# Half tiles filled with zeros at the hybrid mixers' branch projections, and a new order of emptying and outputs at the ends of the hybrid and neighbourhood attentions

## The chip, the cores and the metric

One core of one Trainium2 chip runs the whole program. The time is device microseconds of one execution, median of three: 2294.79 us (2292.48 to 2295.53).

## The reference

One sequence of 256 tokens with 1024 features goes through four transformer layers in fp32. First part: two layers, each a mixer, a cross attention to a memory of 256 tokens and a feed-forward network with a three-tap convolution. The first layer's mixer is the even one (grouped attention and mLSTM), the second layer's the odd one (neighbourhood attention and differential attention). Second part: two layers, each a half-step feed-forward network, a hybrid mixer, a cross attention and another feed-forward network. The change touches the odd mixer and both hybrid mixers:

```python
def odd_mixer(h, w_in, ...):
    qc, kc, vc, qd, kd, vd = split_cols(h @ w_in, OD_SIZES)
    yc = neighbourhood_attention(qc, kc, vc, na_rpb)         # 8 heads of 64
    yd = differential_attention(q12[0], q12[1], k12[0], k12[1], vd, lam, t5_table)
    return concatenate([merge(yc), merge(yd)]) @ w_out

def hybrid_mixer(h, positions, w_in, ...):
    o_fox = fox_attention(fq, fk, fv, log_f)                 # 6 heads of 64: 384 rows
    o_dsa = dsa_sparse_attention(dq, dk, dv, q_idx, k_idx, w_idx, topk)  # 5 heads: 320 rows
    o_sb = stick_breaking_attention(sq, sk, sv)              # 5 heads: 320 rows
    g = sigmoid(gates)
    merged = g[0] * (o_fox @ w_fox_out) + g[1] * (o_dsa @ w_dsa_out) + g[2] * (o_sb @ w_sb_out)
    return merged @ w_out
```

## The kernel before

Activations lie feature by token: a tile is 128 features by 256 tokens. Every matrix product in fp32 is made of three matmuls of parts: the weight is split in a rounded part `whi` and a remainder `wlo`, the activation in `x_hi` and `x_lo`, and the products lo x hi, hi x lo and hi x hi are summed (`product`, L882, L883, L885; in `as_it_comes`, which takes the input tile by tile as it becomes ready, L923, L924, L927). An output tile with eight input tiles is 24 matmuls of 256 columns, one with three input tiles is 9.

Weights come in chunks of up to 2048 columns. SP loads a chunk into one of three `raw` slots (L760) as soon as the slot's former chunk is split; ACT makes `whi` (L1398); `wlo` is a subtraction on DVE (L1843) or, for chunks used inside the attention stages, on POOL (L850, four pieces of 512 columns). A memory chunk is no weight: it replaces the activations `x_hi`, `x_lo` by the normalised memory (ACT L1391, DVE L1839), which must wait until the last unit that reads the old activations is done.

A *unit* is one output of two tiles in one of two PSUM banks, used in turn; unit u may start when unit u-2 has been emptied (`bank_free`). DVE empties gates and queries (L1870), residuals (L1874), tokens (L1861) and the merging of branches (L1879, and the addition L1883 or L1886); ACT empties the memory's keys and values (L1416).

An attention stage is a loop over slots: in slot i PE makes the scores of head group i, then the units that `fill` lists for this slot, the values of group i-2 (L1185) and the transposes of group i-1 (L1171). ACT makes the exponentials of group i (L1641, or the logarithms for the stick-breaking groups), rounds the chunks that `fill` asks for, and copies the transposed probabilities of group i-1 (`back`, L1673). DVE makes maxima and normalisations of group i, then the subtractions and emptyings that `fill` asks for, and last `output(i-2)`: it rounds the attention's output into `x_hi` (L2215) and subtracts into `x_lo` (L2217). Each engine works strictly in this written order. `fill={slot: (end, emptied, ahead)}` means: PE emits units below `end`, the other engines empty units below `emptied`, and chunks are rounded and subtracted up to `ahead` beyond the last unit's (2 where nothing stands).

The hybrid attention has nine groups: 0 to 2 fox, 3 to 5 sparse (dsa), 6 to 8 stick-breaking (sb). Below, F0 to F3 are the units of the fox projection (slots 5 and 6), G9 to G11 the last gates (slots 7 and 8), M0 to M3 those of the dsa projection (slots 9 and 10), S0 to S3 those of the sb projection in the linear stage that follows (`feeds`), W0 to W3 those of `w_out`. dsa and sb have 320 input rows: two whole tiles and a half one of 64 rows. Both halves lie in tile 5 of the output activations, dsa's in rows 0 to 63, sb's in rows 64 to 127, and the matmuls of the half tile contract 64 rows. Each branch has four units of two tiles, so eight output tiles.

In the odd mixer, N0 to N5 are the last units of `od_w_in`, K0 to K3 the memory's keys and values, H0 to H3 the first half of `od_w_out`. K0 comes right after the neighbourhood attention, before a barrier of the stages.

## Time and profile before

| | us |
|---|---|
| median of three | 2294.79 |
| the profiled execution's own time | 2294.97 |
| its span | 2293.2 |
| PE busy | 2203.7 (96%) |
| PE weight load busy | 2112.2 (92%) |
| DVE busy | 1504.9 (66%) |
| ACT busy | 1108.0 (48%) |
| POOL busy | 355.9 (16%) |

The profile is one execution. Busy time is the time in which at least one instruction of an engine runs; the share is an average over stages with quite different limits. The granted clock is the share of TensorE's 2.4 GHz: 1.00 or 0.50 in a stretch. Times of rows are counted from the span's start. In this trace the neighbourhood attention ends at about 547 us, the first hybrid mixer's attention at about 1285 us and the second's at about 1992 us.

### The profile page before, as it was taken

Reading aid. Unit: us, or ns where it says so; the run is one execution under the profiler, and the core shown is the slowest. Engines: PE = TensorE matmul, PEld = TensorE weight load, DVE = VectorE, ACT = ScalarE, POOL = GpSimd, SP = SyncE. Lnnn points to the kernel's source line nnn. Section 1 sums busy time; section 2 is a strip of 40 time slices with the busy share of each in tenths; the row PEclk is TensorE's granted clock in tenths of the full one; section 3 lists DMA queues with packets and bytes.
Section 4 is the critical chain, followed back from the end, with each engine's and each line's share of the span. In section 5 each row is a group of like instructions: output and inputs, shape, how many; then the busy total and the mean of one; then the engine's idle time right before and its main releaser. Section 6 shows DMA issues by size and latency. Waiting matters only on the chain.

```text
span 2293.2 us, 40427 instructions
## 1 busy us (share of the span) xinstructions
PE 2203.7 (96%) x17458; PEld 2112.2 (92%) x17458; DVE 1504.9 (66%) x2210; ACT 1108.0 (48%) x1335; POOL 355.9 (16%) x300
## 2 busy tenths in 40 slices
PE   8988999998799999999999999999999999999998
PEld 7777899997689999999988799999999998799998
DVE  6656787843578787567766657657656566657655
ACT  5345654544465445335646455335334456455333
POOL 2760000055000000000645120000000015320000
PEclk9989999999999999999999999999999999999999
DMA  8653355543245555546643354555555653355552
GB/s 280 181 165 111 111 188 198 176 158 117 92 131 168 200 174 189 189 166 184 195 143 104 124 182 163 195 176 184 184 184 167 175 166 105 117 171 169 185 184 92
DMA packets 316964, 375.13 MB, mean 164 GB/s; under 512 B 27255, under 2 KB 283011, under 8 KB 315635
## 3 DMA queue, kind: packets, MB, share of 16 engines
q1 hardware_dynamic: 311635, 354.88, 47.4%
q0 software_dynamic: 3424, 11.50, 1.8%
q10 hardware_dynamic: 1728, 6.17, 0.7%
q8 instruction: 138, 2.26, 0.4%
q14 instruction: 39, 0.32, 0.0%
HBM read 363.34 MB, written 9.18 MB: 162 GB/s over the span
## 4 chain that ended last, share of the span: by engine, by line
PE 85%; DVE 7%; ACT 3%; issue 2%; DMA 1%; SPq 1%; DVEq 0%; POOL 0%; ACTq 0%
PE banks L882 24%; PE banks L885 23%; PE banks L883 23%; PE banks L923 3%; PE banks L924 3%; PE banks L927 3%; DVE wlo L1843 2%; PE banks L1147 1%; DMA raw<-in_ev_w_in 1%; PE banks L1185 1%; ACT whi L1398 1%; PE banks L1171 1%; PE banks L1045 1%; SPq L760 1%; PE banks L892 0%
## 5 line engine op out<-in xcount | busy, mean ns | idle before, releaser
L882 PE MATMUL banks<-x_hi,wlo 128*128 128x256 f32 (+1 forms) x4344 | 1101.5, 286 | 18.2 <-DVE gt L1879 6.9
L883 PE MATMUL banks<-x_lo,whi 128*128 128x256 f32 (+1 forms) x4344 | 1092.3, 284 | 0.0
L1398 ACT ACTIVATE whi<-raw 128x2048 fp32r<-128x2048 f32 (+3 forms) x340 | 637.7, 1879 | 601.1 <-PE banks L885 551.8
L882 PEld LDWEIGHTS banks<-x_hi,wlo 128*128 128x128 f32 (+1 forms) x4344 | 838.4, 193 | 37.0 <-issue 19.8
L883 PEld LDWEIGHTS banks<-x_lo,whi 128*128 128x128 f32 (+1 forms) x4344 | 839.0, 193 | 0.0
L1843 DVE TENSOR_TENSOR wlo<-raw,whi 128x2048 fp32r<-128x2048 f32 (+4 forms) x290 | 652.3, 2260 | 120.6 <-ACT whi L1398 120.3
L885 PE MATMUL banks<-x_hi,whi 128*128 128x256 f32 x4344 | 687.9, 284 | 0.0
L885 PEld LDWEIGHTS banks<-x_hi,whi 128*128 128x128 f32 x4344 | 595.8, 193 | 3.2
L850 POOL TENSOR_TENSOR wlo<-raw,whi 128x512 fp32r<-128x512 f32 x192 | 251.7, 1347 | 1121.4 <-ACT whi L1398 1121.4
L923 PE MATMUL banks<-x_hi,wlo 128*128 128x256 f32 (+1 forms) x624 | 170.5, 305 | 13.9 <-DVE gt L1879 5.0
L924 PE MATMUL banks<-x_lo,whi 128*128 128x256 f32 (+1 forms) x624 | 163.9, 295 | 0.0
L923 PEld LDWEIGHTS banks<-x_hi,wlo 128*128 128x128 f32 (+1 forms) x624 | 127.6, 204 | 20.8 <-issue 6.1
L2409 DVE TENSOR_TENSOR wk<-banks,norm_scale 128x512 f32<-128x512 f32 x132 | 90.9, 689 | 74.2 <-PE banks L885 69.6
L924 PEld LDWEIGHTS banks<-x_lo,whi 128*128 128x128 f32 (+1 forms) x624 | 127.7, 205 | 0.4
L805 POOL TENSOR_SCALAR gt<-gt,cols 128x256 f32<-128x256 f32 x32 | 42.6, 1343 | 544.8 <-DVE gt L1921 544.8
L2448 DVE CAST x_hi<-wk 128x512 fp32r<-128x512 f32 x66 | 28.2, 427 | 131.6 <-PE banks L885 130.6
L2427 DVE SCALAR_TENSOR_TENSOR wk<-wk,cols 128x255 f32<-128x255 f32 x176 | 73.4, 480 | 39.4 <-ACT wk L1763 38.7
L882 PE MATMUL banks<-whi,x_lo 128*128 128x256 f32 (+3 forms) x400 | 96.7, 282 | 0.0
L883 PE MATMUL banks<-wlo,x_hi 128*128 128x256 f32 (+3 forms) x400 | 95.3, 279 | 0.0
L927 PE MATMUL banks<-x_hi,whi 128*128 128x256 f32 (+1 forms) x632 | 92.9, 285 | 0.0
L1763 ACT ACTIVATE wk<-wk,cols 128x256 f32<-128x256 f32 x88 | 45.7, 590 | 92.0 <-DVE wk L2409 92.0
L1447 ACT ACTIVATE x_hi<-xT,con,cols 128x256 fp32r<-128x256 f32 x112 | 60.9, 590 | 59.7 <-DVE xT L1874 49.8
...
## 6 DMA issues: line engine op xcount, KB each, us to landing
...
```

What stands on the lines that cost most here:

```text
L850: m = eng.tensor_tensor(wlo[s][:, at:at + PIECE], full[:, at:at + PIECE], whi[s][:, at:at + PIECE].bitcast(F32), ALU.subtract)
L882: eng.matmul(out, a[1], b[0], start=first and i == 0, stop=False, skip_group_check=True)
L883: eng.matmul(out, a[0], b[1], start=False, stop=False, skip_group_check=True)
L885: m = eng.matmul(out, a[0], b[0], start=False, stop=last and i == len(operands) - 1, skip_group_check=True)
L923: eng.matmul(bank[:, o], a[1], b[0], start=i == 0 and k0 + k == 0, stop=False, skip_group_check=True)
L924: eng.matmul(bank[:, o], a[0], b[1], start=False, stop=False, skip_group_check=True)
L927: m = eng.matmul(bank[:, o], a[0], b[0], start=False, stop=k == n - 1, skip_group_check=True)
L1398: eng.activation(whi[s % SETS][:, 0:ch["n"]], raw[i % SLOTS][:, 0:ch["n"]], ACT.Copy).then_inc(S["weights_hi"], 1)
L1447: eng.activation(X[nm["buf"]][0][:, k, :], xT[:, k, :], ACT.Identity, scale=cols[:, nm["gain"] + k:nm["gain"] + k + 1], bias=C("zero")).th ...
L1843: eng.tensor_tensor(wlo[s][:, 0:n], full[:, 0:n], whi[s][:, 0:n].bitcast(F32), ALU.subtract).then_inc(S["weights_split"], 1)
L2409: return eng.tensor_tensor(wk[:, half, :].rearrange("p (n c) -> p n c", c=SEQ), bank[:, :].rearrange("p (n c) -> p n c", c=SEQ), norms, AL ...
L2427: m = eng.scalar_tensor_tensor(out=o, in0=wk[:, half, i * SEQ:(i + 1) * SEQ][:, src], scalar=cols[:, w:w + 1], in1=o, op0=ALU.mult, op1=AL ...
```

## The change

Three things are changed. One: in a branch projection with a half tile, the other 64 rows of that weight tile are loaded with zeros (a new input of 64 x 512 zeros, one more DMA per chunk), and the matmuls contract all 128 rows. The dsa units then read rows 64 to 127 of tile 5 too, so they wait for group 6's output (`dsa = n_of["att"] + 7`).

Two: in the hybrid attention DVE empties all units of a slot but the last right after its subtractions and the top-k rounds, ahead of `output(i-2)`; in the last slot `output` comes ahead of the subtractions. In the stage that follows ACT rounds the chunk for W1 ahead of parts 2 and 3, and DVE makes parts 2 to 7 of the merged activations together after S3.

Three: in the neighbourhood attention `output(i-2)` comes ahead of the slot's `fill`, unit N5 moves from slot 2 to slot 3, K0's weights are loaded and rounded ahead of the memory chunk, and in slot 4 ACT copies the transposed probabilities ahead of rounding.

```diff
@@ row_chunk @@
                     pieces.append((v[p0:p0 + r, at, :], w[r0:r0 + r, col:col + n]))
-                    own.append((at, p0, p0 + r))
+                    if r < P:
+                        pieces.append((v[HD - p0:P - p0, at, :], io["zeros"][:, 0:n]))
+                    own.append((at, 0, P))
@@ memory_units @@
-        def memory_units(layer, buf, last_unit):
+        def memory_units(layer, buf, last_unit, keys_first=False):
+            wkv, done = io["ca_w_kv"][layer], COLS if keys_first else 0
+            units = features(wkv, buf, 0, done, 0, "plain")
             c = mem_chunk(layer, buf, last_unit)
-            wkv = io["ca_w_kv"][layer]
-            us = enroll(features(wkv, buf, 0, 512, 0, "plain")) + enroll(values(wkv, buf, 512, 512, 0, "plain"))
+            units += features(wkv, buf, done, 512 - done, done // P, "plain")
+            us = enroll(units) + enroll(values(wkv, buf, 512, 512, 0, "plain"))
@@ odd_mixer, neighbourhood attention @@
-                      fill={0: (N[4], N[3]), 1: (N[5], N[4]), 2: (N[5] + 1, N[5]), 3: (N[5] + 1, N[5] + 1)})
-            K = memory_units(1, b, N[5])
+                      fill={0: (N[4], N[3]), 1: (N[5], N[4]), 2: (N[5], N[5]), 3: (N[5] + 1, N[5], 2), 4: (N[5] + 1, N[5] + 1, 3)})
+            K = memory_units(1, b, N[5], keys_first=True)
             H = enroll(residual_half(wo, o, 0))
-            stages[-1]["fill"][4] = (N[5] + 1, N[5] + 1, 3)
@@ hybrid_mixer @@
-            fox, dsa = n_of["att"] + 3, n_of["att"] + 6
+            fox, dsa = n_of["att"] + 3, n_of["att"] + 7
@@ ACT, linear @@
+                    if feeds is not None and i == 1:
+                        split_upto(two_on(units[2]["chunk"]))
                     if feeds is not None:
                         parts_hi(feeds, 2 * i, 2 * i + 2)
@@ ACT, in_units @@
+                    back_first = st.get("outputs_first") and i == len(units)
+                    if back_first:
+                        back(i - 1)
                     fill(st, i)
-                    if 0 <= i - 1 < len(units):
+                    if 0 <= i - 1 < len(units) and not back_first:
                         back(i - 1)
@@ DVE, linear @@
-                    if feeds is not None and i:
-                        parts_lo(feeds, 2 * i - 2, 2 * i)
+                    if feeds is not None and i in (1, 3):
+                        parts_lo(feeds, i - 1, i + 1)
...
-                    parts_lo(feeds, 6, 8)
+                    parts_lo(feeds, 4, 8)
@@ DVE, in_units @@
+                    outputs_first = st.get("outputs_first") or i > len(units)
+                    if outputs_first and i >= 2:
+                        output(i - 2)
                     fill(st, i)
...
+                    if top and i in st["fill"]:
+                        evac_upto(st["fill"][i][0] - 1)
-                    if i >= 2:
+                    if i >= 2 and not outputs_first:
                         output(i - 2)
```

DVE around G11, M0 and M1 in the second hybrid mixer (the first reads the same), from `output(6)` of 64 rows to M3's merging, before:

```order
L2215 CAST x_hi<-banks 64x256 [waits att_o]
L2217 TENSOR_TENSOR x_lo<-banks,x_hi 64x256 [waits dve_step]
L1870 SCALAR_TENSOR_TENSOR gt<-banks,norm_scale 128x512 [waits mem_stored,lin_ready] x2
L1843 TENSOR_TENSOR wlo<-raw,whi 128x1536 [waits weights_hi]
L2215 CAST x_hi<-banks 128x256 [waits att_o]
L2217 TENSOR_TENSOR x_lo<-banks,x_hi 128x256 [waits dve_step]
L1879 SCALAR_TENSOR_TENSOR gt<-gt,banks 128x512 [waits gated,lin_ready]
L1883 TENSOR_TENSOR gt<-gt 128x512 [waits lin_free]
L1879 SCALAR_TENSOR_TENSOR gt<-gt,banks 128x512 [waits gated,lin_ready,dve_step]
```

And after (the changed kernel's lines 1851, 1878, 1887, 1891, 2223, 2225 are 1843, 1870, 1879, 1883, 2215, 2217 of before):

```order
L1878 SCALAR_TENSOR_TENSOR gt<-banks,norm_scale 128x512 [waits mem_stored,lin_ready]
L2223 CAST x_hi<-banks 64x256 [waits att_o]
L2225 TENSOR_TENSOR x_lo<-banks,x_hi 64x256 [waits dve_step]
L1878 SCALAR_TENSOR_TENSOR gt<-banks,norm_scale 128x512 [waits mem_stored,lin_ready]
L1851 TENSOR_TENSOR wlo<-raw,whi 128x1536 [waits weights_hi]
L1887 SCALAR_TENSOR_TENSOR gt<-gt,banks 128x512 [waits gated,lin_ready]
L1891 TENSOR_TENSOR gt<-gt 128x512 [waits lin_free]
L2223 CAST x_hi<-banks 128x256 [waits att_o,dve_step]
L2225 TENSOR_TENSOR x_lo<-banks,x_hi 128x256 [waits dve_step]
L1887 SCALAR_TENSOR_TENSOR gt<-gt,banks 128x512 [waits gated,lin_ready]
```

G10 is now emptied ahead of `output(6)`, and M0 ahead of `output(7)`.

DVE from the last `output` of the attention to W1's chunk, before (L2012 makes the lo parts of the merged activations):

```order
L1843 TENSOR_TENSOR wlo<-raw,whi 128x1536 [waits weights_hi,dve_step]
L2215 CAST x_hi<-banks 128x256 [waits att_o]
L2217 TENSOR_TENSOR x_lo<-banks,x_hi 128x256 [waits dve_step]
L1843 TENSOR_TENSOR wlo<-raw,whi 128x2048 [waits weights_hi]
```

And after:

```order
L2223 CAST x_hi<-banks 128x256 [waits att_o,dve_step]
L2225 TENSOR_TENSOR x_lo<-banks,x_hi 128x256 [waits dve_step]
L1851 TENSOR_TENSOR wlo<-raw,whi 128x1536 [waits weights_hi]
L1851 TENSOR_TENSOR wlo<-raw,whi 128x2048 [waits weights_hi]
```

`output(8)` passes the subtraction of S2's chunk.

ACT in the neighbourhood attention, from the exponentials of group 1 to the barrier, before (L1641 the exponentials, L1673 `back`, L1391 the memory, L1398 weights):

```order
L1673 ACTIVATE wk<-banks 128x1024 [waits att_pt]
L1641 ACTIVATE wk,stat<-wk,stat 128x256 [waits att_pt,att_max]
L1641 ACTIVATE wk,stat<-wk,stat 128x256 x3
L1673 ACTIVATE wk<-banks 128x1024 [waits att_o,att_pt]
L1641 ACTIVATE wk,stat<-wk,stat 128x256 [waits att_pt,att_max]
L1641 ACTIVATE wk,stat<-wk,stat 128x256 x3
L1673 ACTIVATE wk<-banks 128x1024 [waits att_o,att_pt]
L1391 ACTIVATE x_hi<-raw 128x2048 [waits lin_ready,weights_loaded1]
L1398 ACTIVATE whi<-raw 128x2048 [waits lin_ready,weights_loaded2]
L1398 ACTIVATE whi<-raw 128x2048 [waits lin_ready,weights_loaded0]
L1673 ACTIVATE wk<-banks 128x1024 [waits att_o,att_pt]
```

And after (lines 1646, 1678, 1394, 1401 are 1641, 1673, 1391, 1398 of before):

```order
L1401 ACTIVATE whi<-raw 128x2048 [waits lin_ready,weights_loaded1]
L1678 ACTIVATE wk<-banks 128x1024 [waits att_pt]
L1646 ACTIVATE wk,stat<-wk,stat 128x256 [waits att_pt,att_max]
L1646 ACTIVATE wk,stat<-wk,stat 128x256 x3
L1678 ACTIVATE wk<-banks 128x1024 [waits att_o,att_pt]
L1646 ACTIVATE wk,stat<-wk,stat 128x256 [waits att_pt,att_max]
L1646 ACTIVATE wk,stat<-wk,stat 128x256 x3
L1394 ACTIVATE x_hi<-raw 128x2048 [waits lin_ready,weights_loaded2]
L1678 ACTIVATE wk<-banks 128x1024 [waits att_o,att_pt] x2
L1401 ACTIVATE whi<-raw 128x2048 [waits lin_ready,weights_loaded0]
```

K0's weights stand now three copies earlier, and the last `back` no longer stands behind two roundings of weights.

## Rows read from the trace of the kernel before

**Rows 1.** The page: chain that ended last, by engine.
```profile
PE 85%; DVE 7%; ACT 3%; issue 2%; DMA 1%; SPq 1%; DVEq 0%; POOL 0%; ACTq 0%
```

**Rows 2.** Both hybrid ends and two low-clock stretches: busy by engine, then granted clock (PEclk).
```profile
1941.00:2018.00 77.00, 69.11 (x466) 59.56 (x466) 47.27 (x66) 37.90 (x44) 25.29 (x18) 0.93 0.37 119
1234.00:1311.00 77.00, 68.94 (x464) 59.51 (x465) 47.39 (x66) 37.99 (x44) 25.35 (x18) 0.93 0.35 118
...
2006.80:2013.50 6.70, 5.56 (x27) 5.30 (x26) 5.42 (x10) 3.25 (x5) 0.00 (x0) 0.50 0.48 157
...
545.90:552.70 6.80, 5.24 (x26) 4.84 (x23) 0.85 (x2) 4.35 (x6) 6.80 (x7) 0.50 0.69 227
```

**Rows 3.** Waits, 1941 to 2018 us: us in total, times, longest.
```profile
PE banks L882 <- DVE gt L1879: 3.4, 3, 1.4
...
PE banks L923 <- DVE gt L1879: 2.4, 2, 1.3
...
PE banks L923 <- DVE x_lo L2217: 1.1, 1, 1.1
...
PE banks L882 <- DVE gt L1870: 1.0, 1, 1.0
```

**Rows 4.** Timeline of PE in unit M2: start, us, what; in brackets idle before.
```profile
1985.53 0.28 PE L883 MATMUL banks<-x_lo,whi 128*128 128x256 f32 x1
1985.74 0.38 PE L882 MATMUL banks<-x_hi,wlo 64*128 64x256 f32 x1
1985.96 0.28 PE L883 MATMUL banks<-x_lo,whi 64*128 64x256 f32 x1
1986.08 0.71 PE L885 MATMUL banks<-x_hi,whi 64*128 64x256 f32 x3
...
1987.54 0.71 PE L885 MATMUL banks<-x_hi,whi 64*128 64x256 f32 x3
```

**Rows 5.** Timeline of DVE at the second hybrid end.
```profile
1941.99 1.27 DVE L1879 SCALAR_TENSOR_TENSOR gt<-gt,banks 128x512 f32<-128x512 f32 x2
...
1975.72 1.29 DVE L1870 SCALAR_TENSOR_TENSOR gt<-banks,norm_scale 128x512 f32<-128x512 f32 x2
...
1991.24 0.69 DVE L1879 SCALAR_TENSOR_TENSOR gt<-gt,banks 128x512 f32<-128x512 f32 x1 [1.49 <-PE banks L885]
...
1992.69 1.76 DVE L1843 TENSOR_TENSOR wlo<-raw,whi 128x1536 fp32r<-128x1536 f32 x1
1994.37 0.42 DVE L2215 CAST x_hi<-banks 128x256 fp32r<-128x256 f32 x1
...
2003.33 2.29 DVE L1843 TENSOR_TENSOR wlo<-raw,whi 128x2048 fp32r<-128x2048 f32 x1 [1.92 <-ACT whi L1398]
...
2007.53 0.68 DVE L1879 SCALAR_TENSOR_TENSOR gt<-gt,banks 128x512 f32<-128x512 f32 x1
```

**Rows 6.** Timeline of ACT there: W1's chunk.
```profile
2001.40 1.90 ACT L1398 ACTIVATE whi<-raw 128x2048 fp32r<-128x2048 f32 x1
```

**Rows 7.** Timeline of PE at the neighbourhood attention's end.
```profile
535.26 1.09 PE L1171 MATMUL banks<-con,wk 128*128 128x128 f32 x8
538.77 1.76 PE L1185 MATMUL banks<-wk,vt 128*64 128x256 f32 x8 [2.43 <-ACT wk L1673]
...
545.08 1.26 PE L1185 MATMUL banks<-wk,vt 128*64 128x256 f32 x8 [2.64 <-ACT wk L1673]
```

**Rows 8.** Timeline of PE: first matmul of K0.
```profile
547.89 0.55 PE L882 MATMUL banks<-x_hi,wlo 128*128 128x256 f32 x1 [1.56 <-POOL wlo L850]
```

**Rows 9.** Timeline of ACT there.
```profile
538.62 1.90 ACT L1391 ACTIVATE x_hi<-raw 128x2048 fp32r<-128x2048 f32 x1
540.42 3.70 ACT L1398 ACTIVATE whi<-raw 128x2048 fp32r<-128x2048 f32 x2
```

**Rows 10.** Timeline of POOL there.
```profile
542.40 15.16 POOL L850 TENSOR_TENSOR wlo<-raw,whi 128x512 fp32r<-128x512 f32 x12 [21.53 <-ACT whi L1398]
```

**Rows 11.** The page, DMA issues: KB each, us to landing.
```profile
raw<-in_w_dsa_out SPq DMA_DIRECT2D x4, 128.0 KB, 3.3
```

**Rows 12.** Timeline of SP's queue: both chunks of w_sb_out.
```profile
1962.44 12.23 SPq L760 DMA_DIRECT2D raw<-in_w_sb_out  x6
```

5 lines of the change are left out of this document (3 added, 2 removed).

## The prediction

> **What bounds the kernel now.** I read the chain of waits first: 85% of the path that ended last is PE [rows 1]. PE is the bound nearly everywhere, so a change gains where it shortens PE's own work or closes a gap on PE. I then looked for the three places that the diff touches. The two hybrid ends are alike: in stretches of 77 us PE is busy 69.11 and 68.94 us at a mean granted clock of 0.93 [rows 2], so I work out the second and count it twice. The waits there show what PE stands for: emptyings of PSUM banks by DVE (3.4 us before L882, 2.4 before L923, 1.0 for a gate) and 1.1 us for the attention's last output [rows 3]. At the neighbourhood end PE waits 2.43 and 2.64 us for copies by ACT [rows 7] and 1.56 us for POOL's subtraction of K0's weights [rows 8]; the clock there is 0.50 in 545.9 to 552.7 [rows 2].
>
> **Half tiles.** In M2 the timeline gives the start of each matmul. Among matmuls of one height the next starts 0.12 us later (64 rows after 64 rows: 1985.96 to 1986.08). From 128 to 64 rows it is 0.21 (1985.53 to 1985.74), and the one after that 0.22 [rows 4]. An output tile has nine matmuls and should take 9 x 0.12 = 1.08; it takes 1987.54 - 1986.08 = 1.46. So one tile loses 0.38 us, in two changes of height at 0.19 each. dsa has 8 output tiles: 3.0 us per hybrid. sb has 8 more: another 3.0 of PE time. With zeros every matmul has 128 rows, and a matmul of 64 rows costs the same 0.12 as one of 128, so the added rows cost PE nothing.
>
> The Trainium skill ("TensorEngine Tiling (Array Packing)", Key Properties) says that changing the tiling mode, not just the tile, drains the engine; the trace agrees and gives it the price of 0.19 us. The same page (When to Use Tiling) advises row tiling for a contraction of 64 or less, with up to twice the speed, which speaks against filling up. The trace shows no such gain: the 64-row matmuls follow one another no faster than whole ones. By that rule the sum would lose at most the half of 48 matmuls x 0.12 per hybrid, 2.9 us.
>
> The zeros are 8 more DMAs of 128 KB in all; such a piece lands in 3.3 us [rows 11]. Chunks are issued ahead: the last piece of w_sb's second chunk is issued at 1974.7 (1962.44 + 12.23) [rows 12] for S2, while M0 hasn't begun. Between nothing and 3.3 us of delay per chunk I take nothing; that lead covers even the upper end.
>
> **Emptying ahead of outputs, hybrid.** `output` takes 0.8 us of DVE (two instructions of 0.42, as at 1994.37). F0's emptying starts at 1941.99 behind one [rows 5]; ahead of it F2 starts 0.8 earlier. That alone would be lost, since the logarithms of group 6 don't move, but F2's own emptying passes `output(4)` in the next slot too, so G9 starts 0.8 earlier, and PE is dense from there to group 6's values: 0.8 arrives. M0 started behind G10's emptying, which started at 1975.72 behind `output(6)` [rows 5]. It now needs only `output(6)` itself (the new wait of `dsa + 7`), done at 1975.7: another 0.8. The added wait costs nothing more, for what is queued behind it on PE are M0, M1 and values(7), and all of that starts earlier. M2's gap of 0.87 (the third of those in the first row of [rows 3]) goes: M0 is emptied ahead of `output(7)`. With the 3.0 of dsa, M3 is ready 0.8 + 0.8 + 0.9 + 3.0 = 5.5 us earlier. DVE took it at 1991.24 [rows 5]; now at 1985.7.
>
> **From M3 on DVE sets the pace.** Behind M3 DVE has, in the new order: emptying M3 1.4, `output(8)` 0.8, the subtractions of 1.7 and 2.2, S0 1.4, S1 1.4 (a product and an addition of 0.7 each), two lo parts 0.7, W1's chunk 2.2, S2 1.4, S3 0.7, which is 13.9; I add 0.5 for waiting for ACT's rounding of W1's chunk. That is 14.4. Before it was 2007.53 + 0.68 - 1991.24 = 17.0 [rows 5]. The difference of 2.6 is the wait of 1.92 for ACT, whose rounding started at 2001.40 behind parts 2 and 3 [rows 6], and 0.7 of lo parts that move behind S3. PE's savings in this stretch (3.0 in sb, 1.1 at the last output) don't add: PE finishes S1 about 1.8 us before S0 is empty and S3 about 2 us before S2 is. So what I expect late next is DVE. The W units need all parts only afterwards: PE uses one part in 8 x 0.12 = 0.96 us, DVE makes one in about 0.4 (half of one emptying's 0.69, of the same rate). Gain per hybrid: 5.5 + 2.6 = 8.1, twice 16.2.
>
> **Clock in the hybrids.** Behind the gaps before W0 and W1 the clock is 0.50 for 2006.8 to 2013.5, with 5.56 us of PE work [rows 2], which costs 2.8 (half of it). The new gaps are as long in sum or a bit longer, and one lies in front of S2, where a slow PE is covered by DVE. I take the same cost and bound it at 2 us to either side for each hybrid.
>
> **Neighbourhood end.** N5 goes behind scores(3), and the values of groups 0 and 1 come earlier; PE was dense there until 536.35 (535.26 + 1.09) [rows 7] and has the same work in another order. The memory may be rounded once N5 is done, and N5 now ends ahead of values(1) and these transposes (1.09 each), so ACT's 1.90 us for it [rows 9] lie beside them. values(2) then waits for one copy, about 1.1 us, instead of 2.43. values(3) waited for ACT's copy behind 1.90 and 3.70 us of rounding [rows 9]; with the copy first its gap is about 1 us, not 2.64. K0's weights are rounded in slot 1, and POOL, idle for 21.53 us before its twelve subtractions, four a chunk, from 542.40 on [rows 10], has them ready before slot 3. K0 then waits for the last output alone, about 1.0 us instead of 1.56. The gaps shrink from 6.6 (2.43 + 2.64 + 1.56) to 3.1, by 3.5; and values(2), 1.76 us long where 1.09 is usual [rows 7], and the transposes behind them ran at half clock, which costs some 1.4 less. K0 starts at 543.0 instead of 547.9: 4.9 us. K0 ran from 547.89 to 552.7 at half clock, which cost 2.4 us. With smaller gaps that could vanish or return in a smaller piece. I take 0.6 of it, nearer to its staying, since three gaps of 1 us remain. Sum 5.5; bounds 3 (the low clock stays as long and comes under K0 in full) and 7.3 (it goes).
>
> **Sum.** 16.2 + 5.5 = 21.7 us off 2294.97, the profiled execution's own time (its span is 2293.2, with 1.8 outside): 2273.3. That execution is 0.2 above the median, so the median I predict is 2273.1, rounded to 2273.5 since every slip of my bookkeeping would be towards less.
>
> **Rivals.**
> *The change of height is not what costs* (0.07). If the 0.19 came from the partition range or from the half tile's place, filling would save nothing and M3 is only 2.5 us earlier: 2273.5 + 6 = 2279.5. Against it: both directions cost the same, whichever chunk.
> *The new order passes its gaps on* (0.17). DVE stays late for other reasons, a low clock takes the place of each gap closed, and each end gives about 60% of the sum: 2282. For it: DVE is already the bound behind M3, and low clock followed two gaps of together 2.4 us [rows 3]. Against: the 3.0 of dsa per hybrid is PE work and can't wait elsewhere before M3.
> *The clock recovers* (0.12). With all low stretches gone at the three ends: 2.4 - 0.6 more at K0, 2.8 in each hybrid: 2273.5 - 7.4 = 2266.
> *Slower: the zeros come late* (0.03). SP issues in order, and a chunk counts as loaded only with its zeros. sb's second chunk is issued at 1974.7 [rows 12] and ACT would take it behind the last group's copy, some 7 us later. If the zeros took over 15 us instead of 3.3, the gain of a hybrid would be gone; at 25 us each hybrid loses 7 more than it gains: 2294.8 + 14 - 5.5 = 2303. Nothing in the trace speaks for such a landing time.
> *It doesn't tell* (0.03): within 0.2%, gains and low clock cancelling: 2293.
>
> **Numbers.** The forecast has 0.58; its own range is 2269 to 2278 (2 us of clock for each hybrid, 2 at the neighbourhood end). The range for 8 in 10 takes in the clock's recovery in part and the first rival: 2267 to 2282. A change within 0.2% (4.6 us) can't be told from none here: faster 0.94, same 0.03, slower 0.03.
>
> **What would show it.** In the changed profile: no matmul of 64*128 among L882 to L927, and starts 0.12 apart all through M0 to S3, so that an output tile takes 1.08; PE's wait before M2 gone, and that for x_lo at L923 gone; new waits of PE for DVE of 1 to 2 us before S2 and W0; M3 emptied 5.5 us sooner after group 6's values than before; W1's rounding ahead of the parts 2 and 3. At the neighbourhood end K0's subtraction on POOL some 20 us before its use, and K0's first matmul at about 543 us. I am wrong if the 77 us of a hybrid end shrink by less than 5 or more than 11, or if K0 begins at 543 but the next stage starts no earlier than before.

## The result: 2265.1 us, faster than forecast by 8.4 us

The changed kernel takes 2265.09 us in the median of 4 runs (2264.89 to 2270.05), the kernel before 2294.76 beside it on the same chip (2292.48 to 2295.53). The ratio is 0.9877, 95% interval 0.9862 to 0.9892. The forecast was 2273.5 with a range of 2267 to 2282: the direction was right, the gain of 29.7 us is larger than forecast, and the time lies 1.9 us below the range. The profiled execution took 2264.89 us, its span is 2263.1.

### The profile page after: what moved, and what is told of

Same layout as the page of the kernel before. It is cut to its first block, busy times and chain, and to the rows that moved or that the text cites. A ratio compares the mean times of both kernels' runs of the same rounds, so it can differ in the third digit from the quotient of the medians.

```text
span 2263.1 us, 40437 instructions
## 1 busy us (share of the span) xinstructions
PE 2180.9 (96%) x17458; PEld 2099.1 (93%) x17458; DVE 1509.9 (67%) x2210; ACT 1107.6 (49%) x1335; POOL 356.3 (16%) x300
## 4 chain that ended last, share of the span: by engine, by line
PE 88%; DVE 7%; ACT 3%; issue 2%; DVEq 0%; DMA 0%; ACTq 0%
PE banks L885 24%; PE banks L886 23%; PE banks L888 23%; PE banks L926 3%; PE banks L927 3%; PE banks L930 3%; DVE wlo L1851 2%; PE banks L1150 1%; PE banks L1188 1%; PE banks L1174 1%; PE banks L1048 1%; ACT whi L1401 1%; PE banks L895 0%; PE banks L1239 0%; PE banks L1291 0%
## 5 line engine op out<-in xcount | busy, mean ns | idle before, releaser
L885 PE MATMUL banks<-x_hi,wlo 128*128 128x256 f32 x4344 | 1096.2, 285 | 16.2 <-DVE gt L1887 7.0
L886 PE MATMUL banks<-x_lo,whi 128*128 128x256 f32 x4344 | 1089.0, 284 | 0.0
L1401 ACT ACTIVATE whi<-raw 128x2048 fp32r<-128x2048 f32 (+3 forms) x340 | 637.8, 1878 | 590.2 <-PE banks L888 549.2
L885 PEld LDWEIGHTS banks<-x_hi,wlo 128*128 128x128 f32 x4344 | 837.0, 193 | 31.7 <-issue 20.7
L886 PEld LDWEIGHTS banks<-x_lo,whi 128*128 128x128 f32 x4344 | 837.4, 193 | 0.0
L888 PE MATMUL banks<-x_hi,whi 128*128 128x256 f32 x4344 | 682.2, 283 | 0.0
L926 PE MATMUL banks<-x_hi,wlo 128*128 128x256 f32 x624 | 164.9, 298 | 11.5 <-DVE x_lo L2020 4.9
L927 PE MATMUL banks<-x_lo,whi 128*128 128x256 f32 x624 | 159.5, 290 | 0.0
L926 PEld LDWEIGHTS banks<-x_hi,wlo 128*128 128x128 f32 x624 | 124.2, 199 | 16.8 <-issue 5.6
L927 PEld LDWEIGHTS banks<-x_lo,whi 128*128 128x128 f32 x624 | 124.3, 199 | 0.4
L930 PE MATMUL banks<-x_hi,whi 128*128 128x256 f32 x632 | 91.4, 283 | 0.0
```

The costliest lines, as they stand in the source:

```text
L885: eng.matmul(out, a[1], b[0], start=first and i == 0, stop=False, skip_group_check=True)
L886: eng.matmul(out, a[0], b[1], start=False, stop=False, skip_group_check=True)
L888: m = eng.matmul(out, a[0], b[0], start=False, stop=last and i == len(operands) - 1, skip_group_check=True)
L926: eng.matmul(bank[:, o], a[1], b[0], start=i == 0 and k0 + k == 0, stop=False, skip_group_check=True)
L927: eng.matmul(bank[:, o], a[0], b[1], start=False, stop=False, skip_group_check=True)
L930: m = eng.matmul(bank[:, o], a[0], b[0], start=False, stop=k == n - 1, skip_group_check=True)
```

## The profile after

The page's chain by engine answers to [rows 1]; it is a little more PE than before (85%), and DMA and SP's queue are gone from it.

```profile
PE 88%; DVE 7%; ACT 3%; issue 2%; DVEq 0%; DMA 0%; ACTq 0%
```

The next fence answers to [rows 2]: busy time of PE, PEld, DVE, ACT and POOL, then the granted clock, DMA share and GB/s. The first two rows are 68.6 us of the hybrid ends from group 6's last scores on (in the first hybrid, the second row, that is up to the start of W2; in the second hybrid W2 starts 1.5 us later); the others are three of the stretches at half the clock that are left. Below, such a stretch is called a low stretch.

```profile
1921.60:1990.20 68.60, 62.62 (x485) 57.65 (x485) 50.38 (x67) 38.23 (x45) 25.54 (x18) 0.98 0.44 140
1227.00:1295.60 68.60, 62.61 (x497) 57.65 (x497) 50.52 (x68) 39.70 (x46) 25.59 (x18) 1.00 0.45 142
...
1931.60:1935.00 3.40, 3.29 (x15) 3.32 (x16) 2.47 (x4) 3.34 (x5) 2.99 (x3) 0.50 0.10 28
593.60:597.00 3.40, 3.40 (x11) 2.39 (x10) 1.01 (x3) 1.01 (x2) 0.00 (x0) 0.50 0.00 0
610.60:617.50 6.90, 5.26 (x23) 4.97 (x24) 5.86 (x10) 3.25 (x5) 0.00 (x0) 0.51 0.00 0
```

The clock is 1.00 and 0.98 where it was 0.93: the low stretches behind W1 (1300.2 to 1307.0 and 2006.8 to 2013.6 before) and ahead of it in the first hybrid (1245.6 to 1249.0) are gone, as are both at the neighbourhood end (539.0 to 542.4, 545.9 to 552.7).

PE's timeline in M2 (start, us) answers to [rows 4]: every matmul has 128 rows and the next starts 0.12 us later, also from one output tile to the next; the tile takes 1.07 us (1961.69 to 1962.76).

```profile
1961.69 0.28 PE L886 MATMUL banks<-x_lo,whi 128*128 128x256 f32 x1
1961.81 0.28 PE L885 MATMUL banks<-x_hi,wlo 128*128 128x256 f32 x1
...
1962.28 0.52 PE L888 MATMUL banks<-x_hi,whi 128*128 128x256 f32 x3
1962.64 0.28 PE L885 MATMUL banks<-x_hi,wlo 128*128 128x256 f32 x1
1962.76 0.28 PE L886 MATMUL banks<-x_lo,whi 128*128 128x256 f32 x1
```

PE's waits in the second hybrid end answer to [rows 3]; the wait for x_lo at the first merged tiles is gone, and S2 and W0 wait for DVE, as the prediction expected. The timeline rows behind them give the first hybrid's waits of 1.74 (S2), 1.68 (W0) and 0.61 us (W1).

```profile
PE banks L885 <- DVE gt L1887: 3.5, 3, 1.7
PE banks L926 <- DVE gt L1887: 2.3, 2, 1.7
PE banks L885 <- DVE x_lo L2225: 0.2, 1, 0.2
```

```profile
1276.99 0.35 PE L885 MATMUL banks<-x_hi,wlo 128*128 128x256 f32 x1 [1.74 <-DVE gt L1887]
1283.21 0.35 PE L926 MATMUL banks<-x_hi,wlo 128*128 128x256 f32 x1 [1.68 <-DVE gt L1887]
1284.53 0.36 PE L926 MATMUL banks<-x_hi,wlo 128*128 128x256 f32 x1 [0.61 <-DVE gt L1887]
```

DVE's timeline answers to [rows 5]: M3 is emptied at 1966.13, and the subtraction of W1's chunk (1976.25) waits for ACT 0.60 us instead of 1.92, since ACT rounds W1's chunk at 1974.32, ahead of parts 2 and 3, not behind them as in [rows 6].

```profile
1966.13 0.69 DVE L1887 SCALAR_TENSOR_TENSOR gt<-gt,banks 128x512 f32<-128x512 f32 x1 [0.74 <-PE banks L888]
...
1976.25 2.29 DVE L1851 TENSOR_TENSOR wlo<-raw,whi 128x2048 fp32r<-128x2048 f32 x1 [0.60 <-ACT whi L1401]
...
1979.78 0.68 DVE L1887 SCALAR_TENSOR_TENSOR gt<-gt,banks 128x512 f32<-128x512 f32 x1
```

PE at the neighbourhood end answers to [rows 7, 8]: gaps of 1.11, 1.11 and 0.98 us instead of 2.43, 2.64 and 1.56, and values(2) takes 1.08 us instead of 1.76. (The second row is cut short by the end of its window.)

```profile
537.39 1.08 PE L1188 MATMUL banks<-wk,vt 128*64 128x256 f32 x8 [1.11 <-ACT wk L1678]
540.61 0.65 PE L1188 MATMUL banks<-wk,vt 128*64 128x256 f32 x4 [1.11 <-ACT wk L1678]
542.68 0.38 PE L885 MATMUL banks<-x_hi,wlo 128*128 128x256 f32 x1 [0.98 <-DVE x_lo L2225]
```

To compare kernels I cut each execution at four events on PE: the row sums of the heads stage that opens the neighbourhood attention (491 us), those of the next two such stages, and W1's first matmul in either hybrid (start, us; the row sums go on behind the windows that these rows come from, so only their starts count). The rows of before, then of after:

```profile
491.39 0.60 PE L1045 MATMUL banks<-wk,con 128*16 128x256 f32 x2
555.91 0.60 PE L1045 MATMUL banks<-wk,con 128*16 128x256 f32 x2
609.55 0.60 PE L1045 MATMUL banks<-wk,con 128*8 128x256 f32 x2
1301.44 0.55 PE L923 MATMUL banks<-x_hi,wlo 128*128 128x256 f32 x1 [1.29 <-DVE gt L1879]
2008.36 0.55 PE L923 MATMUL banks<-x_hi,wlo 128*128 128x256 f32 x1 [1.14 <-DVE gt L1879]
```

```profile
491.32 0.39 PE L1048 MATMUL banks<-wk,con 128*16 128x256 f32 x1
548.62 0.39 PE L1048 MATMUL banks<-wk,con 128*16 128x256 f32 x1
602.27 0.60 PE L1048 MATMUL banks<-wk,con 128*8 128x256 f32 x2
...
1980.61 0.36 PE L926 MATMUL banks<-x_hi,wlo 128*128 128x256 f32 x1 [0.61 <-DVE gt L1887]
```

Nothing ahead of 491 us is touched by the change (of the kernels below only e7 and e9 have an edit there). Behind it the stretches A (neighbourhood), B, C (with the first hybrid end), D (W1 to W1) and E (to the end) are, for every profiled execution of this study, worked out in the same way:

```
kernel                         start     A      B       C       D       E    start to end
before                         491.39  64.52  53.64  691.89  706.92  284.84    1801.8
after                          491.32  57.30  53.65  682.26  696.08  282.49    1771.8
after, second time (e14)       485.82  57.30  53.70  683.64  696.16  283.88    1774.7
e1  zeros only                 490.45  65.27  54.61  688.16  703.33  284.88    1796.3
e2  hybrid order only          491.28  64.52  53.68  684.63  698.72  282.47    1784.0
e3  neighbourhood only         497.90  57.29  52.34  691.88  706.97  284.72    1793.2
e4  fillers in before          488.70  63.86  53.68  694.83  702.89  282.54    1797.8
e5  half the height changes    494.93  65.27  54.60  690.25  702.92  284.03    1797.1
e6  after without zeros        487.26  57.29  52.36  684.65  698.71  282.53    1775.5
e7  after, fillers             495.28  57.30  53.67  681.23  695.47  282.45    1770.1
e8  after, idle put back       491.29  57.30  53.66  683.50  698.76  284.69    1777.9
e9  after, fillers moved       483.72  57.28  52.35  681.28  694.65  282.52    1768.1
e10 merging order only         491.23  65.30  54.61  689.48  700.58  282.50    1792.5
e11 outputs' order only        486.96  65.25  53.49  687.04  702.69  284.67    1793.1
e12 fillers, neighbourhood     493.40  63.66  53.75  694.89  706.58  284.52    1803.4
e13 e9 less the first layer's  493.55  57.30  52.33  682.53  694.62  282.47    1769.3
e15 e2 with idle put back      489.38  63.88  53.64  690.56  699.93  282.61    1790.6
```

After against before: 7.2 in A, 9.6 in C, 10.8 in D, 2.4 in E, 30.0 of the 30.1 us between the spans. The first 13 us of D and of E hold nothing of the change but W1's and W0's tiles behind the wait: the same 92 matmuls from W1's first tile to W2 took 13.57 us in the first hybrid and 13.40 in the second before, and take 11.10 now in both. That is clock alone.

```profile
1301.40:1315.00 13.60, 13.56 (x92) 13.59 (x93) 5.13 (x8) 4.66 (x5) 0.00 (x0) 0.79 0.36 123
```

Each row of the table is one execution. A is 57.28 to 57.30 us in all eight executions with the new order of the neighbourhood end and 63.7 to 65.3 in the nine with the old one, so A's gain is 6.4 to 8.0 us. C, D and E move with the low stretches of the execution too: e14 is the same program as after and gained 27.1 us over before from 491 us on, not 30.0.

## The experiments

### The three parts apart (e1, e2, e3) and a filler in the kernel before (e4)

e1 has the zeros alone:

```
+                    if r < P:
+                        pieces.append((v[HD - p0:P - p0, at, :], io["zeros"][:, 0:n]))
-                    own.append((at, p0, p0 + r))
+                    own.append((at, 0, P))
```

> The kernel before with one part of the change: half tiles filled with zeros, and the wait of the dsa units for group 6's output. Theory A (PE pays 0.19 us at each change of contraction height; behind M3 DVE sets the pace): dsa gives 3.0 us per hybrid up to M3, sb 0.5 more (the 0.55 us in which DVE waits for S1 in the profile before), together 7 us over both hybrids: 2288 us, with output tiles at 1.08 us instead of 1.46. Theory B (the added rows cost, or the changes of height are not the price): 2294 or more. If the clock's low stretches behind W0 and W1 go as well (theory C, the clock follows the gaps on PE), up to 5 us more; but their gaps (1.26 and 1.14 us) stay in this kernel, so C expects the low stretches to stay: 2288 too.

Measured: 2287.62 us, ratio 0.9961 (0.9946 to 0.9977). C and D are 3.7 and 3.6 shorter: the 3.0 of dsa, and 0.6 of sb's. The rest of sb's is swallowed: W0 waits 2.99 us for DVE, 1.3 before.

```profile
1296.50 0.36 PE L925 MATMUL banks<-x_hi,wlo 128*128 128x256 f32 x1 [2.99 <-DVE gt L1881]
```

e2 has the hybrid reordering alone (the edits of e10 and e11 below together).

> The kernel before with the hybrid's new order alone (emptying ahead of outputs, the last output ahead of the subtractions, the order of the stage that follows); half tiles stay at 64 rows. Theory A: 0.8 + 0.8 + 0.9 up to M3 and 2.4 behind it, 4.9 per hybrid, 9.8 in all: 2285 us. Theory C: as the gaps move, the low clock of about 6.8 us behind W0 and W1 can go, 2.5 us for each hybrid and 1.4 for one at G9: down to 2279. Rival (gaps are passed on to DVE): 2291 or more.

Measured: 2277.06 us, ratio 0.9915 (0.9900 to 0.9929), where the order alone would give 2285. W1's tiles take 11.10 us in the first hybrid (1294.11 to 1305.21), and D and E say the same of the second: the clock is back with no zeros in the kernel.

e3 has the neighbourhood end alone (N5 a slot later, the last output and copy ahead of the filling units, K0's weights ahead of the memory chunk). As in the whole change, the edit also passes `outputs_first=True` and gives the stage behind it `"pre": (K[1], K[0], 3)` instead of `(K[1], K[0])`, one chunk further ahead; the diff ahead of the prediction does not print the second of these.

```
-                      fill={..., 2: (N[5] + 1, N[5]), 3: (N[5] + 1, N[5] + 1)})
+                      outputs_first=True, fill={..., 2: (N[5], N[5]), 3: (N[5] + 1, N[5], 2), 4: (N[5] + 1, N[5] + 1, 3)})
```

> The kernel before with the neighbourhood end's part alone (outputs first, N5 a slot later, K0's weights ahead of the memory chunk, the last copy ahead of the roundings). In the changed kernel's profile this end came out 7.2 us shorter, K0 starting at 542.7 instead of 547.9 and running at full clock. Theory A with the clock restored: 2287.5 us, the low stretches at 539 and 546 us gone. If the 7 us were partly given back later: over 2289.

Measured: 2287.85 us, ratio 0.9968 (0.9956 to 0.9979). A is 57.29 as in the whole change, 7.2 less, and K0 runs at full clock. C and D are those of before. Its profiled execution, 2291.1 us of span, would have told little: it began its A 6.5 us late.

e4 is the kernel before with matmuls of constants in the gaps ahead of W0 and W1. They compute nothing that is used.

```
                         arrived(chunk_of)
+                        for _ in range(keep[j] if keep else 0):
+                            eng.matmul(banks[2][:, 0:SEQ], C("add128"), C3("causal")[:, 0, :], start=True, stop=True)
                         before()
```

> The kernel before, unchanged in order, with two more matmuls of constants into an idle bank just ahead of each of the waits for the emptying of S2's and S3's banks (units W0 and W1), in both hybrids: PE is busy for about 1 us of each gap of 1.26 and 1.14 us, and nothing else changes. Theory C (the low clock in 2006.8 to 2013.5 comes from PE's idle gaps just before): the low stretch goes and 2.5 us per hybrid are won with the same schedule: 2290 us. Rival D (the low clock there comes from something else, as DMA or DVE load, or from the gaps' length in sum over a longer time): no gain, or 0.5 us slower, 2295.

Measured: 2288.66 us, ratio 0.9980 (0.9967 to 0.9992). More work, less time. In the first hybrid W1's stretch is at full clock, which the windows view shows (columns as above):

```profile
1301.00:1312.30 11.30, 11.23 (x93) 11.23 (x94) 5.33 (x9) 4.78 (x5) 0.00 (x0) 1.00 0.45 154
```

So the clock there is a cost of its own, which hangs on what PE does in its gaps. W1's tiles are low in all ten hybrid ends of the kernels with the old order and no filler there (before, e1, e3, e5, e12) and full in both of e4. In C e4 loses 2.9 us again, to a low stretch at 650.7 to 657.5 that before doesn't have; e9, e12, e13, e15 and e14, the unedited changed kernel, have one there too, so it goes with the execution and not with an edit.

### Is it the change of height that costs? (e5)

The kernel before; in M0 to M3 the 64-row matmuls of neighbouring output tiles stand side by side.

```
+                short = [p for p in operands if p[0][0].shape[0] < P]
+                if short and odd is not None:
+                    tall = [p for p in operands if p not in short]
+                    ... all three matmuls of each pair, for half in ((short, tall) if odd else (tall, short))
```

> The kernel before, with one thing changed: in the branch units of the hybrid attention stage (not in the two that open the merging stage) the nine matmuls of an output tile are ordered so that the three of 64 rows stand last in the first and third tile and first in the second and fourth. The same matmuls run, on half as many changes of contraction height: one for each output tile instead of two. If a change of height is what costs 0.19 us, the units M0 to M3 go from 6.04 to about 5.28 us, an output tile in them from 1.46 to about 1.27, and the kernel saves 1.5 to 1.8 us in each hybrid: 2291.5 us against 2294.8. If a matmul of 64 rows is itself slow, the units stay at 6.04 us and the time at 2294.8.

Measured: 2288.69 us, ratio 0.9980 (0.9971 to 0.9989). M0 and M1 together, four output tiles, take 5.28 us (1977.74 to 1983.02) instead of 6.07, as the first theory said. Six 64-row matmuls follow one another at 0.12, and each change of height shows as two steps of 0.2 (1978.61 to 1978.84; 1979.31, 1979.52, 1979.74):

```profile
1978.61 0.38 PE L888 MATMUL banks<-x_hi,wlo 64*128 64x256 f32 x1
1978.84 0.28 PE L888 MATMUL banks<-x_lo,whi 64*128 64x256 f32 x1
1978.96 0.28 PE L888 MATMUL banks<-x_hi,whi 64*128 64x256 f32 x1
1979.07 0.28 PE L888 MATMUL banks<-x_hi,wlo 64*128 64x256 f32 x1
...
1979.31 0.28 PE L888 MATMUL banks<-x_hi,whi 64*128 64x256 f32 x1
1979.52 0.38 PE L888 MATMUL banks<-x_hi,wlo 128*128 128x256 f32 x1
1979.74 0.28 PE L888 MATMUL banks<-x_lo,whi 128*128 128x256 f32 x1
```

C and D give 1.6 and 4.0; the excess of 2.4 in D is clock (no low stretch at G9 of the second hybrid, a shorter one behind W1 of the first).

### What the zeros are worth in the whole change (e6)

The diff is e1's, taken back in the changed kernel.

> The changed kernel with the half tiles left at 64 rows: both reorderings, no zeros. With the kernel that had the hybrid reordering alone, the stretch from the last scores of the hybrid attention stage to W1 took 61.2 us, with the whole change 58.6, so 2.6 us come back in each hybrid: 2265.1 plus 5.3, 2270.4 us. If the price of the zeros is the same with and without the reordering (6.2 us by the medians of the kernel with zeros alone), 2271.3. If their worth in the whole change was to keep the clock up, low-clock stretches ahead of W1 come back and it is 2275.

Measured: 2266.4 us, ratio 0.9888 (0.9873 to 0.9903), 1.3 above the changed kernel. C and D say 2.4 and 2.6: with the DVE work in its new order the zeros end in longer waits of S2 and W0 (1.74 and 1.67 instead of 0.22 and 0.16). In the profiled executions the start (487.26) and B, 1.3 shorter by the place of a low stretch, hide this: the spans are 0.3 apart. The medians rest on four executions each, and the intervals of the two ratios overlap widely; they don't tell 1.3 us from 5.0. No low clock came back in the profiled execution: nothing shows that the zeros carry it.

### Idle put back into the changed kernel (e8)

```
                     g, acc = gt[:, 8 * b + t:8 * b + t + 2, :], gt[:, t:t + 2, :]
+                    for k in range(2 if (b, t) == (2, 6) else 0):
+                        eng.tensor_tensor(gt[:, 8 + 4 * k:10 + 4 * k, :], gt[:, 10:12, :], gt[:, 10:12, :], ALU.add)
```

> The changed kernel with two more 128x512 additions on VectorE (0.69 us each, into tiles that nobody reads any more) ahead of the emptying of S3, so that W1 waits about 1.4 us longer in each hybrid. If the clock is the separate term that the prediction left out, a gap of 2.0 instead of 0.6 us ahead of W1 may bring back the low clock of W1 to W3: 1.4 for the wait and 2.4 for the clock in each hybrid, 2272.7 us, with stretches at half the clock at about 1285 and 1982. If the gain in W1 to W3 came with the order itself, 2265.1 plus 2.8, 2267.9, and no such stretch.

Measured: 2266.91 us, ratio 0.9884 (0.9871 to 0.9898); its profiled execution took 2271.03, the others 2264.7 to 2267.9. In the profiled one W1 waits 1.81 and 1.82 us, and its tiles run at 0.87 and 0.80 of the clock:

```profile
1285.70:1298.40 12.70, 12.65 (x93) 12.68 (x94) 5.88 (x10) 4.73 (x5) 0.00 (x0) 0.87 0.38 120
1984.50:1997.50 13.00, 12.99 (x90) 13.00 (x91) 5.58 (x9) 4.32 (x4) 0.00 (x0) 0.80 0.34 114
```

Two waits longer by 1.2 us each and 1.5 and 2.2 us of clock make 6.1 in all, as between the spans. Whether the low clock is in the other three executions is not known: their mean granted clocks are 0.986, 0.986 and 0.990 against 0.987 in the profiled one, and their totals move with the first 491 us too.

### The hybrid reordering taken apart (e10, e11)

e10, the merging stage's order alone:

```
+                    if feeds is not None and i == 1:
+                        split_upto(two_on(units[2]["chunk"]))
...
-                    if feeds is not None and i:
-                        parts_lo(feeds, 2 * i - 2, 2 * i)
+                    if feeds is not None and i in (1, 3):
+                        parts_lo(feeds, i - 1, i + 1)
...
-                    parts_lo(feeds, 6, 8)
+                    parts_lo(feeds, 4, 8)
```

> The kernel before with the reordering of the merging stage alone: the weights of S2 rounded behind S0's and S1's emptying, and two of the subtractions for W0 moved behind S3's. The outputs at the end of the attention stage stay behind the subtractions, so the gaps of 1.12, 0.99, 0.87 and 1.06 us stay as they are. By the steps of the prediction 2.6 us less behind M3 in each hybrid, of which S0's wait may keep some: 1.5 to 2.6 each. If the clock of W1 to W3 hangs on the two gaps next to it, it recovers and gives 2.4 more in each: 2294.8 less 8 to 10, 2286. If it hangs on the sum of the gaps in the tens of us before, low clock stays: 2290 to 2292.

Measured: 2284.7 us, ratio 0.9962 (0.9948 to 0.9977). From the last scores to W1 2.3 less in the first hybrid, and 2.4 in the second beside a clock effect of 1.5: the 2.6 of the prediction nearly in full. The waits ahead of W0 and W1 shrink to 0 and 0.20, and W1's tiles are at full clock in both hybrids, though the waits of 1.12, 0.99, 0.87 and 1.06 us further ahead all stay.

```profile
1300.60:1311.80 11.20, 11.18 (x93) 11.20 (x94) 5.87 (x10) 4.75 (x5) 0.00 (x0) 1.00 0.50 166
```

e11, outputs and emptying at the attention's end alone:

```
+                    outputs_first = i > len(units)
+                    if outputs_first and i >= 2:
+                        output(i - 2)
...
+                    if top and i in st["fill"]:
+                        evac_upto(st["fill"][i][0] - 1)
```

> The kernel before with the other half of the hybrid reordering alone: the last two outputs of the attention stage ahead of the subtractions, and emptying ahead of the outputs at the earlier steps. The waits of 1.12 (F2), 0.99 (M0) and 0.87 us (M1) go, 0.8 plus 0.8 plus 0.9, 2.5 in each hybrid, 5.0 in all; the merging stage as before, with 1.3 and 1.1 us ahead of W0 and W1. Without a change of the clock 2289.8. If the gaps at F2, M0 and M1 are what brings W1 to W3 down, 2285, and no stretch at half the clock at about 1300 and 2005.

Measured: 2284.31 us, ratio 0.9959 (0.9947 to 0.9971). The waits of F2, M0, M2 (which the expectation calls M1) and S0 shrink; what arrives at W1 is 3.7 us for each hybrid by D (4.2, of it 0.5 clock), more than the 2.5 forecast: without the zeros the 1.1 at S0 arrives too. The low clock behind W1 stays:

```profile
1292.70:1305.80 13.10, 13.06 (x92) 13.09 (x93) 5.13 (x8) 4.66 (x5) 0.00 (x0) 0.83 0.38 130
```

### Is it the last wait? (e15)

W1's tiles had run slow where W1 itself waited long (1.29 before, 0.80 in e11, 1.81 in e8). e15 is e2 with e8's two additions.

> The kernel with the hybrid reordering alone, and in it two more 128x512 additions on VectorE ahead of the emptying of S3: waits of about 0.2, 0.2 and 1.8 us ahead of S2, W0 and W1, 2.2 us in all, where the changed kernel with 1.74, 1.67 and 0.61, 4.0 us in all, kept its clock. If the last wait decides, W1 to W3 take 12.6 to 13.6 us instead of 11.1, in both hybrids: from 491 us to the end 1784.0 plus 2.4 for the waits and 3 to 5 for the clock, 1789.4 to 1791.4. If the sum decides, the clock stays full there and it is 1786.4.

Measured: 2281.75 us, ratio 0.9947 (0.9933 to 0.9962). From 491 us on it took 1790.6 us, the number of the last-wait theory, and for the wrong reason: W1's tiles run at full clock behind a wait of 1.82 us in both hybrids. The total was made up by low clock elsewhere (593 to 658 us, and at 1245.3).

```profile
1297.46 0.35 PE L923 MATMUL banks<-x_hi,wlo 128*128 128x256 f32 x1 [1.82 <-DVE gt L1883]
```

```profile
1297.40:1308.60 11.20, 11.14 (x93) 11.17 (x94) 5.87 (x10) 4.71 (x5) 0.00 (x0) 1.00 0.39 131
1997.40:2008.50 11.10, 11.10 (x93) 11.10 (x94) 5.76 (x10) 4.67 (x5) 0.00 (x0) 1.00 0.40 129
```

So no single wait decides. All waits from the last scores to W1 in the first hybrid sum to about 8 us before, 10 in e1, 7 in e8 and 9 in e5, all with low clock behind, and to 6.0 in after, 5.7 in e10 and 4.0 in e15 at full clock. But e11 has 4.3 and low clock, and e14 (below) has after's 6.0 and both.

The waits ahead of W0 and W1 alone, added up, sort the ends better. They are 0.2 to 2.0 us in e2, e6, e10 and e15, with full clock in all eight ends, and 0.4 to 1.4 beside fillers in e4, e9 and e13, full in all six. They are 2.3 in after, e7 and e14, full in five ends of six. They are 2.3 to 4.3 in before, e1, e3, e5, e8 and e11, and W1's tiles are at least partly low in all twelve. The two ends of e12 are low with 2.1, but there the low stretch begins at W0's first matmul, and the slower PE shortens the wait ahead of W1. This sorting was found afterwards, no run tested it, and at 2.3 us both outcomes occur, so what tips the clock is not settled.

### A filler where the clock was to recover at the neighbourhood end (e12)

The kernel before with four such matmuls ahead of values(2) and of values(3).

```
+                    if un.get("tables") and i >= 2:
+                        eng.wait_ge(S["att_done"], u - 1)
+                        for _ in range(4):
+                            eng.matmul(ob[i % 2][:, 0:SEQ], C("add128"), C3("causal")[:, 0, :], start=True, stop=True)
```

> The kernel before with four constant fp32 matmuls (1.9 us) in each of the two gaps of 2.43 and 2.64 us ahead of the last two values of the neighbourhood attention, nothing else. Clock theory: K0, which ran at half the clock for most of its 8.1 us, takes 6.0 as in the changed kernel, and the transposes between the gaps 1.1 instead of 2.0; 2 to 3 us less, 62 us from the heads stage at 491 us to the next one instead of 64.5: 2292.3. If K0's clock came with the shorter waits of the reordering itself, 64.5 us and 2294.8.

Measured: 2294.68 us, ratio 1.0001 (0.9988 to 1.0013): no gain. K0 starts as late as before after 491 us (56.5 us), as ACT's copies set it; one of two low stretches is left (549.3 to 552.8), K0 is 0.9 us shorter, and A 63.66 instead of 64.52. But e4 and e15, which have before's code here, took 63.86 and 63.88 for the same stretch, so 0.9 us is no more than executions differ by. In the gap before values(3) 2.47 us are left behind the filler:

```profile
542.71 1.89 PE L1179 MATMUL banks<-con 128*128 128x256 f32 x8
547.08 1.08 PE L1189 MATMUL banks<-wk,vt 128*64 128x256 f32 x8 [2.47 <-ACT wk L1677]
549.90 0.55 PE L882 MATMUL banks<-x_hi,wlo 128*128 128x256 f32 x1 [1.74 <-POOL wlo L850]
```

K0's clock came back in full only with the shorter waits of the reordering. The low time there, 3.5 us, is the shortest of the nine executions with the old order (6.9 to 10.2 in the others), which speaks for the filler theory but doesn't show it.

### Fillers in the changed kernel (e7, e9, e13), and the changed kernel again (e14)

e7 puts constant matmuls into gaps of the first two layers and ahead of G9, through one helper:

```
+            def keep(n, u=None):
+                u = emitted[0] if u is None else u
+                bank_free(u)
+                for _ in range(n):
+                    eng.matmul(lin_bank[u % 2][:, 0:SEQ], C("add128"), C3("causal")[:, 0, :], start=True, stop=True)
```

> The changed kernel with constant fp32 matmuls (128x128 by 128x256, some 0.5 us each, into a bank of the linear units that is free) in gaps that TensorE idles in anyway: two ahead of G9 in each hybrid, and in the first two layers eight or three ahead of the last scores of a dual attention, four ahead of its last turn, five ahead of the spread of the norms in the second layer, five or two ahead of the first merged tiles. Clock theory (a low granted clock follows the gaps and goes with them): the stretches at 1931.6, at 593.6 and 610.6, and those at about 153 and 201 of the changed kernel go; of their 27 us at half the clock some 20 hold matmuls, so up to 9 us come back: about 2257 us, at least one of the stretches of 593.6 to 617.5 gone. Rival (the clock in these places does not hang on what TensorE does in its gaps): 2265, or up to 2268 where a filler ends later than the gap.

Measured: 2266.95 us (2259.67 to 2270.32), ratio 0.9878 (0.9862 to 0.9894). All low stretches from 244 us to the last microseconds go, but only 1.7 us of time. The row shows why: ahead of G9 the gap is the wait for that very bank, and the filler runs behind it, and G9's first matmul comes 0.78 us after the filler's (1239.92).

```profile
1239.14 1.13 PE L940 MATMUL banks<-con 128*128 128x256 f32 x4 [1.36 <-DVE gt L1905]
```

e9 uses the next output's bank there, moves the four of the second layer to the turn that waits, and adds three ahead of S2 and two ahead of W0:

```
+                    eng.wait_ge(S["att_done"], st["u0"] + 4)
+                    for _ in range(2):
+                        eng.matmul(st["ob"][1][:, 0:SEQ], C("add128"), C3("causal")[:, 0, :], start=True, stop=True)
```

> The changed kernel with fillers again, put where the trace of the first attempt says: the two ahead of G9 go into the bank of the next output, which no emptying guards, so that they run in the gap and not behind it; the four of the second layer stand ahead of the last turn but one, where the gap of 2.81 us is; three ahead of S2 and two ahead of W0 are added, and those of the first attempt that ran inside their gaps stay. Clock theory, counted from the heads stage at 491 us on (what comes before varies by up to 10 us between profiled executions of these kernels): the first attempt gained 1.6 us there and lost 1.1 in each hybrid and 1.9 in the second layer to fillers that ended late, so 5.7 us now, 1766.1 us from there to the end against 1771.8; median about 2259.5. If the fillers still delay what follows, 2265. No stretch at half the clock after 491 us but the last one.

Measured: 2255.91 us (2253.59 to 2259.45), ratio 0.9836 (0.9822 to 0.9851): the fastest kernel of the study. The same filler now lies in the gap, and G9 starts when it would have:

```profile
1225.56 1.08 PE L971 MATMUL banks<-con 128*128 128x256 f32 x4
1227.18 0.35 PE L885 MATMUL banks<-x_hi,wlo 128*128 128x256 f32 x1 [0.55 <-DVE gt L1912]
```

From 491 us on it takes 1768.1 us, 3.7 less than after where 5.7 were expected: the misplaced fillers of e7 had cost 0.8 us in D and 1.3 in B, not 1.1 and 1.9, and in C one low stretch is left at 636.1. The rest of the 9.2 us between the medians is not found behind 491 us in the profiled executions.

e13 is e9 without the first layer's fillers, e14 the changed kernel once more.

> The changed kernel with the second attempt's fillers, but without those of the first layer (eight ahead of the third scores of its dual attention, five ahead of the first merged tiles). From the heads stage at 491 us to the end as in the second attempt, 1768.1 us against 1771.8 of the changed kernel. If the rest of the 9 us between those two kernels was the first layer's fillers, the median is 3.7 us under the changed kernel's beside it, about 2261.4; if it came from how the first 491 us happen to run, it can be anything from 2255 to 2268, and 1768 us stay.

> The changed kernel once more, nothing edited. If what differs in the first 491 us goes with the program, the median is 2265.1 again and the heads stage starts at 491.3; if it goes with the execution, both differ. From that stage to the end 1771.8 us, with W1 to W3 at full clock in both hybrids.

Measured: e13 2260.64 us (2258.94 to 2264.62), ratio 0.9858 (0.9844 to 0.9873); e14 2263.86 (2262.27 to 2270.17), ratio 0.9875 (0.9858 to 0.9892). Behind 491 us e13 takes 1769.3, 2.5 less than after and 5.4 less than e14; its median is 3.2 below e14's, with intervals that overlap, so the later fillers' worth is shown by the stretches and not by the medians. e14 repeats after's time and A, but its profiled execution started the neighbourhood 5.5 us sooner, the low stretch at G9 of the first hybrid is back (1232.0 to 1235.4, 1.5 us), and W1's tiles of the second hybrid ran at 0.88 behind after's very waits, with 1.00 in the first:

```profile
1280.40:1291.60 11.20, 11.14 (x93) 11.17 (x94) 5.87 (x10) 4.78 (x6) 0.00 (x0) 1.00 0.53 173
1976.60:1989.00 12.40, 12.38 (x93) 12.40 (x94) 5.80 (x10) 4.71 (x6) 0.00 (x0) 0.88 0.46 155
```

So the changed kernel's full clock is near its edge. Whether the first layer's fillers are worth the remaining 4.7 us between e13 and e9 is open: e7 has them too, and started at 495.28.

## Why the prediction was right and where it failed

- **Half tiles.** Right: 0.38 us for an output tile, and by e5 the price is the change of height, 0.19 us for each. The zeros land 3.1 us after their issue (the row below, of the DMA view of 1900 to 1990 us), and no wait for a chunk shows. Alone they gave 3.6 us for each hybrid (e1) instead of 3.0, in company 2.5 (e6). The Trainium skill ("TensorEngine Tiling (Array Packing)", Key Properties) says that a change of the tiling mode drains TensorE; e5's trace agrees in that each change of height has a price.

```profile
raw<-in_zeros SPq DMA_DIRECT2D x4, 128.0 KB, 3.1
```

- **Emptying ahead of outputs.** F2 starts 0.8 us earlier (wait 0.33 instead of 1.12), M0 another 0.8 (0.18 instead of 0.99), M2 doesn't wait. From the last scores to M3's emptying it takes 5.7 us less against 5.5 forecast.
- **DVE sets the pace behind M3.** Right: waits of 1.74 and 1.67 us ahead of S2 and W0 (1 to 2 forecast), M3's emptying to S3's 14.3 us by DVE's rows (1966.13 to 1979.78 and 0.68) against 14.4. With clock left out the hybrids gave 8.2 and 8.4 us, 8.1 forecast.
- **Neighbourhood end.** K0 starts 5.1 us earlier against 4.9; its gaps sum to 3.2 against 3.1. The 1.4 us put down to half clock in values(2) and the transposes was right only as arithmetic: in e10 and e15 values(2) has the full clock and K0 starts no sooner (56.65 us behind the heads stage, 56.50 in before), because the wait ahead of values(3) grows from 2.64 to 4.20 us. What moved K0 is that ACT's copies come sooner.
- **Clock: the step that failed.** "I take the same cost and bound it at 2 us to either side for each hybrid", and 0.6 at K0. In place of 0.6 us in all the clock gave 8.4: 2.1 in K0 (8.0 to 5.9 us), 1.5 in G9 of the first hybrid (7.4 to 5.9), 2.5 and 2.3 in W1's tiles. Schedule 21.7 (21.1 forecast) and clock 8.4 make the 30.0 measured. In e14, the same program again, the clock gave about 5.5: nothing in G9, and 1.0 instead of 2.3 in the second W1. So part of the 8.4 is the luck of the profiled execution; with 5.5 the same sum would give about 2268, just inside the range, while the medians of both sets of four executions, 2265.1 and 2263.9, lie below it.

The rival "the clock recovers", 2266 with a chance of 0.12, is the nearest to what happened, though not quite by its own sum: it has no low stretch at G9, one of which went in after, and one stayed.

Three things in the reasoning were wrong. First, "the new gaps are as long in sum or a bit longer" counts the wait ahead of S2 with those ahead of W0 and W1. These two fell from 2.6 and 2.4 us to 2.3, and e10 and e11 say that they matter more than the ones further ahead: e10 takes them to 0.2 and leaves the rest, with full clock; e11 takes 3.5 us off F2, M0, M2 and S0, and the clock stays low. Why 2.3 us was enough in three ends of after's code and not in the fourth is open. Second, the list of low stretches was not complete: the stretch at G9 (1245.6 to 1249.0 and 1952.2 to 1955.6 before), worth 1.5 us where it goes, stands in no term. Third, each place was bounded on its own by 2 us, and even these bounds, 6 us in all, were narrowed to 2269 for the forecast's own range. The range should have reached to the case in which the low stretches at all three ends go, and that case deserved far more than 0.12. e4 shows that the clock is a term that can be bought back apart from any wait, e2 and e10 which edit bought it back in the hybrids.
